# The norm between two blocks: RMS from weighed sums, both norms in one pass, and an unrolled layer loop

## The reference

```
for l in range(2):                                   # first block
    x = layer_norm(ALPHA*x + 0.5*swiglu(x, ffn1), ln_f1)
    x = layer_norm(ALPHA*x + token_mixer(x), ln_mix)     # two attentions, gates, projections
    x = layer_norm(ALPHA*x + 0.5*swiglu(x, ffn2), ln_f2_g, ln_f2_b)
hn = rms_norm_2(x, mix_norm_g)                       # second block
proj = hn @ w_in                                     # 19 tiles of 128 columns
x = x + concat(gated linear attention, convolution, differential attention) @ w_out
x = x + hier_moe(rms_norm_2(x, ffn_norm_g))          # 16 experts, two per token
```

## Time and profile before

| | |
|---|---|
| median of three runs (lowest to highest) | 3119.53 us (3115.71 to 3126.17) |
| the profiled execution | 3125.87 us |
| its span, first to last instruction | 3123.7 us |
| mean granted TensorE clock | 0.972 |
| PE busy | 2954.7 us, 95% |
| DVE, ACT, POOL busy | 1510.9, 1221.0, 1168.5 us |
| DMA | 324.21 MB, mean 104 GB/s |

### The profile page before, as it was taken

One profiled execution on the slowest core, in us unless ns is written; L12 is line 12 of the kernel. 1 busy time (PEld: TensorE's weight loads), 2 busy tenths in 40 slices (PEclk: granted clock), 3 DMA queues, 4 the chain that ended last, 5 costly groups with the idle time before them and its releaser, 6 DMA issues.

```text
span 3123.7 us, 38832 instructions
## 1 busy us (share of the span) xinstructions
PE 2954.7 (95%) x13601; PEld 2362.0 (76%) x13601; DVE 1510.9 (48%) x2629; ACT 1221.0 (39%) x1860; POOL 1168.5 (37%) x602
## 2 busy tenths in 40 slices
PE   6999999888999999999999988899999998998997
PEld 5888877657788888888878766778888877675765
DVE  4442365455654413444155544664431469556665
ACT  3332233556343322433232365534332342534653
POOL 3444352421454443544443341235444342111221
PEclk9999999999999999999999999999999999789998
DMA  4333232202423332233323210232333121115995
GB/s 131 94 94 115 80 124 72 68 18 61 128 77 100 96 107 80 88 94 100 109 98 95 85 41 24 89 107 87 101 102 102 53 71 61 34 50 198 361 355 202
DMA packets 118548, 324.21 MB, mean 104 GB/s; under 512 B 12432, under 2 KB 48656, under 8 KB 117904
## 3 DMA queue, kind: packets, MB, share of 16 engines
q1 hardware_dynamic: 108992, 305.17, 30.2%
q10 hardware_dynamic: 2800, 8.91, 0.8%
q0 software_dynamic: 6624, 8.41, 0.8%
HBM read 313.52 MB, written 24.64 MB: 108 GB/s over the span
## 4 chain that ended last, share of the span: by engine, by line
PE 38%; issue 36%; POOL 17%; DVE 7%; ACT 2%; DMA 1%; POOLq 0%; SPq 0%; DVEq 0%; ACTq 0%; another core or an unknown queue 0%
POOL wlo L2687 15%; PE ps L426 6%; PE ps L427 6%; PE ps L429 6%; PE ps L461 3%; PE ps L1991 3%; PE ps L946 2%; PE ps L1977 1%; PE ps L1979 1%; PE ps L1978 1%; DVE cacc L2251 1%; POOL xlo L804 1%; PE ps L1963 1%; PE ps L934 1%; PE ps L844 1%
## 5 line engine op out<-in xcount | busy, mean ns | idle before, releaser
L2687 POOL TENSOR_TENSOR wlo<-raw,whi 128x1024 fp32r<-128x1024 f32 (+1 forms) x368 | 954.0, 2593 | 1493.3 <-ACT whi L583 1493.2
L583 ACT ACTIVATE whi<-raw 128x1024 fp32r<-128x1024 f32 (+1 forms) x368 | 409.4, 1113 | 744.2 <-PE ps L429 656.5
L426 PE MATMUL ps<-xlo,whi 128*128 128x512 f32 x1704 | 666.8, 391 | 6.8 <-DVE sg L1323 4.6
L427 PE MATMUL ps<-xhi,wlo 128*128 128x512 f32 x1704 | 664.4, 390 | 0.0
L429 PE MATMUL ps<-xhi,whi 128*128 128x512 f32 x1704 | 420.8, 389 | 0.0
L426 PEld LDWEIGHTS ps<-xlo,whi 128*128 128x128 f32 x1704 | 320.8, 188 | 75.9 <-POOL wlo L2687 6.8
L427 PEld LDWEIGHTS ps<-xhi,wlo 128*128 128x128 f32 x1704 | 320.7, 188 | 66.0
L429 PEld LDWEIGHTS ps<-xhi,whi 128*128 128x128 f32 x1704 | 319.9, 188 | 66.4
L426 PE MATMUL ps<-hlo,whi 128*128 128x512 f32 x704 | 277.3, 394 | 0.0
L427 PE MATMUL ps<-hhi,wlo 128*128 128x512 f32 x704 | 275.5, 391 | 0.0
L693 DVE SCALAR_TENSOR_TENSOR xa<-ps,xa 128x512 f32<-128x512 f32 x48 | 33.1, 690 | 388.1 <-PE ps L429 388.1
(11 more groups left out here) (577 smaller groups left out, 4932.9 us busy)
## 6 DMA issues: line engine op xcount, KB each, us to landing
raw<-in_gu SPq DMA_DIRECT2D x176, 512.0 KB, 3.6
raw<-in_mix SPq DMA_DIRECT2D x96, 512.0 KB, 3.7
mraw<-in_w SPq DMA_DIRECT2D x23, 2048.0 KB, 12.4
raw<-in_dn SPq DMA_DIRECT2D x64, 704.0 KB, 4.0
mdraw<-in_w SPq DMA_DIRECT2D x23, 1024.0 KB, 13.2
raw<-in_w SPq DMA_DIRECT2D x32, 512.0 KB, 3.6
gate_rows<-tails SPq DMA_DIRECT2D x32, 256.0 KB, 4.2
sgmn<-gate_rows SPq DMA_DIRECT2D x16, 512.0 KB, 4.2
```

The lines of the kernel that those rows point to most:

```text
L426: nc.tensor.matmul(out, whi[:, slot, cols], rlo, start=first and t == 0, stop=False)
L427: nc.tensor.matmul(out, wlo[:, slot, cols], rhi, start=False, stop=False)
L583: nc.scalar.activation(whi[:, s, 0:n], raw[:, r, 0:n], ACT.Copy).then_inc(hi_done, 1)
L2687: nc.gpsimd.tensor_tensor(wlo[:, s, 0:n], raw[:, r, 0:n], whi[:, s, 0:n].bitcast(F32), ALU.subtract).then_inc(w_ready, 1)
```

## The change

Three things are changed. First, in the last layer's second feed-forward (`last`) DVE accumulates, beside the adds, three weighed tiles: the sum over tiles of g^2 x, of g b x and of g^2 x^2 (`weigh`, `weigh_square`), and PE's token sums are extended by the sums of these tiles and, for the eighth tile, by further columns; the means of g^2, g b and b^2 come from one matmul of 24 columns. From these `dve_mean_square` works out the second mean square on [128, 4] numbers. Second, `dve_double_norm` applies both norms to each tile before it goes to the next: shift, bias by ACT into `xa`, scale by the second norm into a ring of four (`squares`), ACT rounds to `xhi`, POOL alone makes `xlo`, while PE multiplies the first pair. The rounds of squares, pair sums and the second sync are gone, and so is the first norm's `xhi` and `xlo`. Third, the loop over the two layers is a Python loop: every engine's program holds both layers, and waits outside the inner loops have constants. In the diff below the loop's first lines are PE's (those of SP, POOL, ACT and DVE read the same), the first loop over `KT + 1` stands in ACT's program, and the last loop in POOL's.

```
-        with pe.Fori(0, DEPTH) as L:
+        for L in range(DEPTH):
...
+        def weigh(m):
+            if last:
+                for k, x in enumerate((gain_sq, gain_bias)):
+                    if m == 0:
+                        own.link(nc.vector.tensor_scalar(weighed[:, k, :], xa[:, m, :], x[:, m:m + 1], None, ALU.mult))
+                    else:
+                        own.wait(own.n if k == 0 else own.n - 1)
+                        own.link(nc.vector.scalar_tensor_tensor(out=weighed[:, k, :], in0=xa[:, m, :], scalar=x[:, m:m + 1],
+                                                               in1=weighed[:, k, :], op0=ALU.mult, op1=ALU.add))
+        def weigh_square(n):
+            if last:
+                if n == 1:
+                    own.link(nc.vector.tensor_scalar(weighed[:, 2, :], sq_sum, gain_sq[:, 0:1], None, ALU.mult))
+                own.wait()
+                own.link(nc.vector.scalar_tensor_tensor(out=weighed[:, 2, :], in0=sq_one, scalar=gain_sq[:, n:n + 1],
+                                                       in1=weighed[:, 2, :], op0=ALU.mult, op1=ALU.add))
...
         pe.wait_ge(S["squared"], KT)
-        sums(ps[3], 0, sq_one).then_inc(S["pair_used"], 1)
-        pe_idle(1)
+        if last:
+            sums(ps[3], 0, sq_one, last_cols[:, 0:2], 2).then_inc(S["pair_used"], 1)
+            pe.wait_ge(S["weighed"], N_WEIGHED)
+            sums(ps[0], 8, weighed[:, 0, :])
...
         pe_spread(ps[6], stat[:, 124:128])
+        if last:
+            for k in (1, 2):
+                ins = sums(ps[0], 8 + 4 * k, weighed[:, k, :])
+            ins.then_inc(S["pair_used"], 1)
...
     def pe_second(pe):
-        pe_squares(pe)
-        sync_point(pe, "pe", lambda: pe_idle(9))
+        pe.wait_ge(S["r_ready"], 1)
+        pe_spread(ps[3], rms2)
+        pe_idle(6)
...
+        for m in range(KT + 1):
+            if m < KT:
+                act.wait_ge(S["tn_ready"], m + 1)
+                nc.scalar.activation(xa[:, m, :], tn[:, m % 2, :], ACT.Identity, bias=pr("ln2b", m)).then_inc(xa_ready, 1)
+            if m >= 1:
+                act.wait_ge(S["hn_ready"], m)
+                nc.scalar.activation(xhi[:, m - 1, :], squares[:, (m - 1) % 4, :], ACT.Copy).then_inc(S["norm_act"], 1)
...
+    def dve_double_norm(dve, own):
+        ver = 3 * DEPTH - 1
+        dve_mean_square(dve, own)
+        for m in range(KT + 1):
+            if m < KT:
...
+                nc.vector.scalar_tensor_tensor(out=tn[:, m % 2, :], in0=ps[6][:], scalar=pr("ln2g", m), in1=xa[:, m, :],
+                                               op0=ALU.mult, op1=ALU.add).then_inc(S["tn_ready"], 1)
+                if m + 2 < KT:
+                    nc.vector.scalar_tensor_tensor(out=xa[:, m + 2, :], in0=xa[:, m + 2, :], scalar=pr("ln2g", m + 2),
+                                                   in1=ps[7][:], op0=ALU.mult, op1=ALU.mult).then_inc(S["norm_dve"], 1)
+            if m == 0:
+                dve.wait_ge(S["var_ready"], 1)
+                nc.vector.reciprocal(rms2, rms2).then_inc(S["r_ready"], 1)
+            if m >= 1:
+                k = m - 1
...
+                nc.vector.scalar_tensor_tensor(out=squares[:, k % 4, :], in0=xa[:, k, :], scalar=p2("mixg", k), in1=ps[3][:],
+                                               op0=ALU.mult, op1=ALU.mult).then_inc(S["hn_ready"], 1)
...
+        for m in range(KT):
+            pool.wait_ge(S["norm_act"], m + 1)
+            nc.gpsimd.tensor_tensor(xlo[:, m, :], squares[:, m % 4, :], xhi[:, m, :].bitcast(F32), ALU.subtract
+                                    ).then_inc(S["zs_ready"], 1)
```

More of the change, by code:

```diff
@@ L151, in program @@
     shift = sb("shift", T, at=R0 + 92 * KB)
+    weighed = sb("weighed", 0, at=xhi_at, shape=[P, 3, T])
     def c(name, rows=P, r0=0):
@@ L223, in program @@
     stat = small[:, 128:256]
+    gain_sq, gain_bias, bias_sq = [small[:, 8 + 8 * k:16 + 8 * k] for k in range(3)]
+    last_cols, gain_means = stat[:, 40:43], stat[:, 44:47]
     gq = sb("gq", T, at=at(0))
@@ L519, in pe_ffn, with pe_shift, pe_stats, sums @@
             if m == 4:
-                pe_shift(pe)
-    def pe_shift(pe):
+                pe_shift(pe, last)
+    def pe_shift(pe, last=False):
         pe.wait_ge(S["own2"], 5)
+        if last:
+            nc.tensor.matmul(ps[5][:, 0:24], c("ones"), small[:, 8:32], start=True, stop=True)
         nc.tensor.matmul(ps[2][:], c("ones"), zs[:], start=True, stop=True).then_inc(S["stat_ready"], 1)
-    def pe_stats(pe, t0):
-        def sums(bank, c0, x):
+    def pe_stats(pe, t0, last=False):
+        def sums(bank, c0, x, cols=c("ones")[:, 0:1], n=1):
             for qt in range(QT):
-                ins = nc.tensor.matmul(bank[:, c0 + qt:c0 + qt + 1], x[:, qt * P:(qt + 1) * P], c("ones")[:, 0:1],
+                ins = nc.tensor.matmul(bank[:, c0 + n * qt:c0 + n * qt + n], x[:, qt * P:(qt + 1) * P], cols,
                                        start=True, stop=True)
@@ L714, in dve_residual @@
         nc.vector.tensor_scalar(shift[:], ps[2][:], 2.0, None, ALU.mult).then_inc(S["own2"], 1)
+        if last:
+            own.link(nc.vector.tensor_reduce(gain_means.unsqueeze(2), ps[5][:, 0:24].rearrange("p (k m) -> p k m", k=3),
+                                             AX_X, ALU.add))
+            own.wait()
+            for k, (by, plus) in enumerate(((0.5, 0.0), (-1.0, 0.0), (1.0, RMS_EPS))):
+                own.link(nc.vector.tensor_scalar(gain_means[:, k:k + 1], gain_means[:, k:k + 1], by, plus, ALU.mult, ALU.add))
         dve.wait_ge(S["own2"], 6)
@@ L728, in dve_residual @@
         dve.wait_ge(S["centred"], 5)
+        for m in range(5):
+            weigh(m)
         added(5)
+        weigh(5)
         nc.vector.tensor_tensor(zs[:], xa[:, 4, :], xa[:, 5, :], ALU.add).then_inc(S["own2"], 1)
@@ L738, in dve_residual @@
         gather(6)
+        weigh(6)
+        assert not last or own.n == N_WEIGHED, own.n
         dve.wait_ge(S["own2"], 11)
@@ L770, in dve_stats @@
         dve.wait_ge(S["r_whole"], 2)
+        if last:
+            dve.wait_ge(S["pair_used"], 4)
     def dve_rstd(dve, bank=ps[3]):
@@ L2836, in _ @@
             one(0, G_FFN1, 0, j)
-        with pool.Fori(0, DEPTH) as L:
+        for L in range(DEPTH):
             for g, follow, k in ((G_FFN1, G_MIX, 0), (G_FFN2, G_LAYER, 2)):
@@ L2882, in _ @@
         act.wait_ge(const_in, 32)
-        with act.Fori(0, DEPTH) as L:
+        for L in range(DEPTH):
             def norm(b):
@@ L2921, in _ @@
         dve.sem_inc(S["tile_free"], 2)
-        with dve.Fori(0, DEPTH) as L:
+        for L in range(DEPTH):
             dve.wait_ge(xa_ready, L * (3 * KT) + KT)
```

125 lines of the change are left out of this document (76 added, 49 removed).

## The result

The changed kernel took 3102.11 us in the median of six runs (3098.11 to 3107.09) against 3118.73 us for the kernel before (six runs, 3109.33 to 3128.82): ratio 0.9935, 95% interval 0.9915 to 0.9955. The forecast was 3103.7 us. Other sets of runs of the two kernels unchanged gave medians of 3115.67 to 3118.01 us for before and 3098.76 for after, so that the median came within 1.6 us of the forecast is in part luck.

The account below looks back on a forecast made before the run. TensorE (PE) was taken as the bound, busy 2954.7 of 3123.7 us, with gains only where it idles or runs fillers. Terms -14.6 - 1.5 + 0.3 = -15.8 us off the 3119.53 median gave 3103.7 us; 8-in-10 range 3093 to 3114.

Parts of the forecast that it names:

- The seam: From the last layer's end to the second block's first pair of products: pair ends at 2502.3, not 2516.91; -14.6 us.
- step 1: Seam, token sums: four sums of the first weighed tile replace a filler, so the spreads begin 0.15 us later.
- (3): Seam, PE: eight more sums that DVE waits for, 3.4 us at the lower clock, 2.1 at the full one.
- (5): Seam, DVE: RMS from the sums in 11 small operations at 0.20 us, 2.2 us; bounds 1.8 to 5.5.
- (6): Seam, DVE: 512-wide operations 0.66 us apart, two and a reciprocal, then two more; first scaled tile at 2486.8.
- (7, 8): Seam, first pair: DVE's three operations a tile, 1.97 us; then ACT rounds, POOL subtracts, PE closes at 2502.3.
- The weighing: Last feed-forward, DVE: 21 wide operations fit its waits, free 2.7 us before add 7, cost 0; PE's added matmul +0.3 us.
- The jump: PE's jump from layer 0 to layer 1: unrolled, the first product starts at 1251.6 instead of 1253.78; -1.5 us.
- A: Rival, seam: clock stays low through the first pair, matmuls 0.43 us apart, gain only 7.0 us, total 3111.3; chance 0.09.
- B: Rival, DVE between adds 5 and 7: weighing makes add 7 31.3 us late, total 3135.0; chance 0.05.
- C: Rival, double norm: small chain and tile pace at upper bounds, no jump gain, -9.3 us, total 3110.2; chance 0.09.
- D: Rival, unrolling: attention's register work saves 3 us more, sums at full clock 1.3 more, total 3099.4; chance 0.15.

Follow-up runs that it names:

- before_again: The kernel before, unchanged, in a second profiled execution: 3124.52 us.
- unroll_only: The kernel before with the layer loops of all five engines unrolled and nothing else: 3117.36 us, ratio 0.9995.
- before_filled: The kernel before with 16 unread matmuls of 256 columns in PE's 3.95 us hole in the second block's differential attention: 3116.54 us, ratio 0.9991.
- after_again: The changed kernel, unchanged, in a second profiled execution: 3100.07 us.
- after_timed: The changed kernel, unchanged, timed beside the others of a later set: 3098.76 us, ratio 0.9932.
- after_delayed: The changed kernel with nine unread matmuls of 256 columns among the second block's first products, so the attention comes later: 3102.12 us, ratio 0.9945.
- after_filled: The changed kernel with 16 unread matmuls of 256 columns in PE's hole in the second block's differential attention: 3098.76 us, ratio 0.9934.
- norms_apart: The changed kernel with the layer norm finished on all eight tiles before the second norm's scaling starts: 3113.10 us, one time.
- no_weigh: The changed kernel with 18 of the 21 wide weighing operations on DVE left out: 3112.96 us, one time.
- prescale: The changed kernel with the first scaling of tiles 2 to 6 put into DVE's wait for the eight weighed sums: 3107.15 us, ratio 0.9956.
- cover_used: The changed kernel with ten more wide weighing-type DVE operations between the last weighed sum and add 7: 3106.03 us, one time.
- prescale_filled: The changed kernel with five early scalings and 16 unread matmuls in PE's hole in the second block's differential attention: 3098.20 us, ratio 0.9942.

## Why the prediction was right, point by point

**The seam.** Counted from add 7's start, us:

| step | forecast | after |
|---|---|---|
| spreads begin (step 1) | 4.4 | 4.47 |
| spreads end (2) | 6.4 | 6.42 |
| eight sums end (3) | 9.8 | 9.62 |
| first small operation (4) | 10.6 | 10.56 |
| small chain ends (5) | 12.8 | 12.4 |
| first scaled tile (6) | 15.7 | 15.06 |
| pair ends (7, 8) | 31.2 | 30.65 |

The eight sums at half clock (3.41 us), the small steps of 0.2 us, 1.97 us a tile and DVE as the steady engine came as forecast. The gain was 15.15 us (45.80 - 30.65) for 14.6. It holds from one execution to the next: the kernels with the old seam took 45.8, 46.2, 45.8 and 46.4 us (before, before_again, unroll_only, before_filled), those with the new one 29.9 to 30.9 (after, after_again, after_timed, after_delayed, after_filled).

**The weighing.** Forecast: DVE free 2.7 us before add 7, cost 0. After: 2.69 us. Without the weighing add 7 waits for the same product; with ten operations more it is late. The forecast price of a two-tile operation held by a POOL split (up to 2.9 us) is what made the cover small. The matmul of 24 columns on PE, forecast at 0.3 us, cost 0.23: add 7 lies 106.92 us behind the first down product's add, 106.69 in unroll_only.

**The jump.** 1251.84 for 1251.6, and 1.1 us left of the forecast 1.5; unrolled alone 1.2. The term that was off is the close of the pair: it ends 1.22 us behind POOL's last tile (1262.78 to 1264.00), not 0.7. Against before_again the gain would have been 3.1, and the forecast did not see that the clock can fall behind this gap. The Trainium skill, "Runtime: NRT & Kernel Launch", Instruction fetch mechanics, says that a taken branch to code outside the fetched pages stalls for a fetch, and gives this as one reason to unroll. The trace agrees in the time of PE's one far jump (3316 ns); that a fetch took it no run shows, and the unrolled kernel's time is 0.9995 of the looped one's.

**The rivals.** A: no, the pair's matmuls start 0.23 us apart at a clock of 1.00; it shows in norms_apart, behind a longer gap. One argument against it did not carry: a gap of 2.24 us left the clock at 1.00 in before, but one of 2.41 did not in before_again. B: no, by 2.7 us, with the mechanism shown. C: no, steps 5 and 7 came at their forecast. D: no for the register work, by the traces of layer 1; the sums stayed at half clock. Two slips in the working change nothing: 17 operations of 0.74 us are 12.6 us, not 12.7, and the start of the pair under A, 2489.3, follows from no row.

**What the forecast had not seen.** The profiled execution was 10 us faster than the sum, all in the attention. One of the prediction's own signs of being wrong thus came, an attention stage of another length; it named D or the longer code for it, and unroll_only, with the longest stage of all profiled executions (108.4 us), shows that the unrolling does not shorten it. The stage's length (first to last score product) goes with its time at half clock, whatever the kernel:

| execution | stage, us | at half clock, us |
|---|---|---|
| before, before_again, unroll_only | 108.0, 102.6, 108.4 | 51.2, 40.4, 58.0 |
| no_weigh, norms_apart, prescale | 102.5, 102.6, 102.5 | 40.7, 40.6, 37.5 |
| after, after_again, after_timed | 95.1, 95.0, 95.4 | 20.5 each |
| cover_used, after_delayed | 95.0, 94.8 | 20.5 each |
| before_filled, prescale_filled | 94.6, 93.7 | 6.8, 3.4 |
| after_filled | 106.3 | 34.1 |

A kernel with the old seam has the short stage once its hole is filled (before_filled; none of the three with the hole open had it), and kernels with the change can have the long one (no_weigh, norms_apart, prescale, after_filled), so the sums and the double norm alone do not bring these 8 to 13 us. In the runs the split is uneven: a mean clock of 0.973 or less in 22 of 68 runs of before, in 4 of 8 of prescale and in none of 22 of after and after_delayed, of which three lie at 0.974, at 3106 to 3108 us. At one and the same mean clock, 0.977, fifteen runs of before average 3114.5 us and four of after 3101.5, 13.0 apart. So of the medians' 16.6 to 19.3 us some 13 to 16 are seam and jump, by this and the filled kernels, and the rest, up to some 6, goes with the clock of that stage. Why after has the short stretch in all its profiled executions stays open. In the eleven executions whose hole is open, the drop came 44.7 to 45.2 us behind the stage's first product where it lasted 34.1 us (three), 45.8 and 46.0 where it lasted 58.0 and 47.8, 46.2 to 47.4 where it lasted 17.1 (five), and 47.7 where it lasted 30.7: each length came with places of its own, but what sets the place was not found.

## What to carry to other kernels

Work out a seam as a chain from one anchor, with durations from rows of the same shape and the clock level that such work had before, and count the cover of what is added on a waiting engine operation by operation, holds by other engines included; here the 2.7 us of cover came out to a tenth. Before a difference between two profiles is booked to a change, compare the granted clock stage by stage and take a second execution: one stage of short matmuls moved by 13 us here without being touched. And a local gain of 2 us (prescale) can vanish behind such a stage, so look at the stage and the total.

## What the runs showed of the hardware

Ahead of the hole that starts the stretch, one tiny operation is held. In after's timeline of all engines, with that line's eight operations (ns minimum/median/maximum) below:

```profile
2679.81 2.86 POOL L2780 TENSOR_TENSOR wlo<-raw,whi 128x1024 fp32r<-128x1024 f32 x1 [7.96 <-ACT whi L591]
...
2680.58 2.12 DVE L2395 TENSOR_SCALAR small<-small 128x2 f32<-128x2 f32 x1
...
2686.38 1.23 PE L891 MATMUL ps<-vd,pt 128*128 128x128 f32 x4 [3.93 <-ACT pt L911]
...
L2395 DVE TENSOR_SCALAR small<-small x8: 228/228/2115, 2658.2 to 2741.0; 128x2 f32<-128x2 f32 x8
```

A DVE operation on two columns takes 2.12 us and ends at 2682.70, 0.03 behind POOL's split; the median of the eight is 0.23, so it is held for 1.9 us, about half the length of the hole (3.93). DVE's finishing steps and the next unit's scores queue behind it, ACT waits for DVE, PE for ACT, and the clock falls (0.79 in 2684 to 2686, 0.50 behind it). The Trainium skill, "SBUF — State Buffer", Terms, says that DVE and GpSimd arbitrate for one shared port pair that is held for a whole instruction; the row agrees, on an operation that has a single tensor input. That removing this one hold would shorten the hole was not tried.
